# Attention of both layers reordered among its projections, and each weight unit's low half used last

## What is computed

```python
for i in range(2):
    h = rms_norm(x, attn_norm[i])
    c_q, c_kv, k_r, q_d, k_d, v_d, g_mla, g_dil = split(h @ w_in[i])
    o_mla = mla_attention(...)        # 8 heads, low-rank q and kv, rotary
    o_dil = dilated_mixer(q_d, k_d, v_d)   # 3 groups x 8 heads of 64, ALiBi
    merged = (sigmoid(g_mla) * (o_mla @ w_br_mla[i]) + sigmoid(g_dil) * (o_dil @ w_br_dil[i]))
    x = x + merged @ w_out[i]
    h = rms_norm(x, ffn_norm[i])
    x = x + (swiglu(h, ...) if i == 0 else moe_swiglu(h, ...))   # d_ff 3584; 8 experts, top 2
    h = rms_norm(x, ple_norm[i])
    x = x + sigmoid(h @ ple_w_gate[i]) * (p[i] @ ple_w_proj[i])
return rms_norm(x, final_norm)
```

## Time and profile before

| | |
|---|---|
| three runs | 2065.55 us median (2065.05 to 2072.18) |
| the profiled execution | 2059.12 us, of which the span of instructions 2057.4 us |
| mean granted TensorE clock | 0.959 |
| busy over the span | PE 95%, DVE 73%, ACT 60% |

### The profile page before, as it was taken

The page is one execution under the profiler, slowest core; times in us unless marked ns, Lnnn a source line. Parts: engine busy times, 40 slices in busy tenths (PEclk is TensorE's granted clock), DMA queues, the critical chain, the costliest instruction groups (busy, mean ns, idle before and its releaser), DMA issues.

```text
span 2057.4 us, 27403 instructions
## 1 busy us (share of the span) xinstructions
PE 1961.5 (95%) x9278; PEld 1633.5 (79%) x9278; DVE 1497.9 (73%) x1685; ACT 1242.8 (60%) x1543; POOL 68.5 (3%) x127
## 2 busy tenths in 40 slices
PE   6998999999999999999899999999999999999996
PEld 5887877788887887877688888888888888888875
DVE  4456447556666455545698999989999898998985
ACT  4545354444445544443577777777777777777764
POOL 2200001000001100001000000000000000000000
PEclk8999899999999997799799999999999999999998
DMA  6543114555554542124499998989989898998980
GB/s 252 192 183 110 54 62 169 194 183 183 184 183 167 213 160 75 42 81 141 185 359 349 352 369 329 367 338 353 371 324 366 339 355 342 352 368 340 351 324 31
DMA packets 70064, 498.61 MB, mean 242 GB/s; under 512 B 7872, under 2 KB 7872, under 8 KB 10096
## 3 DMA queue, kind: packets, MB, share of 16 engines
q1 hardware_dynamic: 68656, 493.39, 63.8%
q0 software_dynamic: 1344, 4.36, 0.7%
HBM read 496.67 MB, written 1.05 MB: 242 GB/s over the span
## 4 chain that ended last, share of the span: by engine, by line
PE 90%; DVE 3%; ACT 3%; issue 3%; DMA 1%; POOL 1%; ACTq 0%; DVEq 0%; SPq 0%; POOLq 0%
PE ps L1425 27%; PE ps L1427 26%; PE ps L1426 26%; PE ps L1562 2%; PE ps L1705 2%; PE ps L1544 1%; PE ps L1713 1%; DVE lo L925 1%; PE ps L1510 1%; ACT hi L554 1%; PE ps L1555 1%; PE ps L1533 0%; PE ps L1522 0%; ACT pT L682 0%; ACT pr L672 0%
## 5 line engine op out<-in xcount | busy, mean ns | idle before, releaser
L925 DVE TENSOR_TENSOR lo<-raw,hi 128x1024 fp32r<-128x1024 f32 (+1 forms) x936 | 1104.8, 1219 | 237.4 <-ACT hi L554 235.6
L554 ACT ACTIVATE hi<-raw 128x1024 fp32r<-128x1024 f32 (+1 forms) x936 | 969.1, 1053 | 395.3 <-PE ps L1427 381.6
L1425 PE MATMUL ps<-hi,hs_hi 128*128 128x512 f32 x896 | 360.6, 402 | 6.9 <-DVE lo L925 5.4
L1425 PE MATMUL ps<-hi,hT_hi 128*128 128x512 f32 (+1 forms) x832 | 344.2, 414 | 21.4 <-DVE lo L925 14.5
L1427 PE MATMUL ps<-hi,hs_lo 128*128 128x512 f32 x896 | 352.5, 393 | 0.0
L1426 PE MATMUL ps<-lo,hs_hi 128*128 128x512 f32 x896 | 349.9, 391 | 0.0
L1426 PE MATMUL ps<-lo,hT_hi 128*128 128x512 f32 (+1 forms) x832 | 335.9, 404 | 0.0
L1427 PE MATMUL ps<-hi,hT_lo 128*128 128x512 f32 (+1 forms) x832 | 335.3, 403 | 0.0
L1425 PEld LDWEIGHTS ps<-hi,hT_hi 128*128 128x128 f32 x832 | 166.8, 200 | 57.6 <-DVE lo L925 11.9
L1425 PEld LDWEIGHTS ps<-hi,hs_hi 128*128 128x128 f32 x896 | 169.1, 189 | 42.7 <-DVE lo L925 8.8
L1427 PEld LDWEIGHTS ps<-hi,hs_lo 128*128 128x128 f32 x896 | 168.9, 188 | 39.6
(11 more groups left out here) (270 smaller groups left out, 1866.4 us busy)
## 6 DMA issues: line engine op xcount, KB each, us to landing
raw<-in_stream SPq DMA_DIRECT2D x468, 1024.0 KB, 4.8
xs<-in_x SPq DMA_DIRECT2D x2, 512.0 KB, 7.0
gain<-in_ffn_norm POOLq DMA_DIRECT2D x2, 512.0 KB, 3.7
gain<-in_ple_norm POOLq DMA_DIRECT2D x2, 512.0 KB, 6.1
out_x<-hnat SPq DMA_DIRECT2D x4, 256.0 KB, 2.3
gain<-in_attn_norm SPq DMA_DIRECT2D x1, 512.0 KB, 5.2
pnat<-in_p POOLq DMA_DIRECT2D x2, 256.0 KB, 3.2
gain<-in_attn_norm POOLq DMA_DIRECT2D x1, 512.0 KB, 6.4
```

The lines of the kernel that those rows point to most:

```text
L554: a.activation(dst, src, ACT.Copy).then_inc(hi_done, 1)
L925: v.tensor_tensor(dst, src, h, ALU.subtract).then_inc(lo_done, 1)
L1425: pe.matmul(o, ah, wh[:, kk, :], start=(first and kk == 0), stop=False)
```

## The change

1. **Low half last.** `unit` waits for `hi_done`, does hi x hi and the low activation half for all k-tiles and blocks, then waits for `lo_done` and does the matmuls with the low weight half. The number of matmuls is the same.
2. **Attention reordered.** The six MLA batches move in between the units of the last three q/k groups, two per group, in banks of their own (scores 2 and 3, probabilities 7). These three groups now all use banks 0 and 1, and the rounds from 6 on use 4 and 5 alone. Of the gate and branch units, three stand ahead of the dilated loop and 16 in it, one in every dilated step but one (`FILL_AT`), where the MLA output is transposed (`OM_AT`). All gates use the bank pair 2 and 3. `exps(n)` waits for `normalise(n - 4)`, since `sums` has four places.
3. **Branches and merge.** The MLA branch units are fillers, the dilated output is transposed in two halves, the additions of the merge go from GpSimd to DVE (`merge`), and `w_out` starts when the first half of the merged rows is ready.
4. **Aligned regions.** `region` rounds its start up to 128 bytes. `omT`, `odT` and `merged` lie at other offsets.

```diff
-EV_OPS = [2] * 7 + [4, 4] + [2] * 9
-GATE_BANKS = (3, 7)
-BRANCH_BANKS = ((2, 6), (0, 1))
+EV_OPS = [2] * 7 + [4, 4] + [2] * 10
+GATE_BANKS = (2, 3)
+BRANCH_BANKS = ((2, 3), (0, 1), (6, 7), (2, 3))
...
-GATE_AT = {n + 2: n for n in range(4)}
-GATE_AT.update({NB_M + 2 + 2 * k: 4 + k for k in range(8)})
-GATE_AT[NB + 1] = 12
-
-SPLIT_AT = {2: 1, NB_M + 4: 2, NB_M + 8: 3}
+FILL_AT = {n: n - 3 for n in range(NB_M, NB_M + 13)}
+FILL_AT.update({NB_M + 14 + k: 16 + k for k in range(3)})
+OM_AT = NB_M + 13
+
+SPLIT_AT = {NB_M + 1: 1, NB_M + 4: 2, NB_M + 8: 3}
...
         def region(n):
+            top[0] = (top[0] + 127) // 128 * 128
...
-        sums = sb("sums", [P, 2, 4])
+        sums = sb("sums", [P, 4, 4])
...
                 def exps(n):
                     a.wait_ge(y.smax, n + 1)
-                    if n >= 2:
-                        a.wait_ge(y.oev, n - 1)
+                    if n >= 4:
+                        a.wait_ge(y.oev, n - 3)
...
+                for j in range(3, 6):
+                    u, n = b + U_Q + 4 * j, 2 * (j - 3)
+                    split_to(u + 6, **kw)
+                    exps(n)
+                    if n:
+                        pt_evac(n - 1)
+                    split_to(u + 7, **kw)
+                    chunk_evac(j)
+                    split_to(u + 8, **kw)
+                    exps(n + 1)
+                    pt_evac(n)
...
+                for n in range(NB_M, NB + 1):
+                    x = FILL_AT.get(n - 1, 0)
+                    if x % 4 == 3 and x < 16:
+                        gate_evac(x // 4, ACT.Copy, y.ev_act)
+                    if n < NB:
+                        exps(n)
+                    if n > NB_M:
+                        pt_evac(n - 1)
...
             def unit(u, dyn, l_hi, l_lo, dims, k0, outs, c0, first, last):
 
                 nk, w = dims
-                pe.wait_ge(lo_done, dyn + u + 1 + LO0)
+                pe.wait_ge(hi_done, dyn + u + 1)
...
                         pe.matmul(o, ah, wh[:, kk, :], start=(first and kk == 0), stop=False)
-                        pe.matmul(o, ah, wl[:, kk, :], start=False, stop=False)
-                        ins = pe.matmul(o, al, wh[:, kk, :], start=False, stop=(last and kk == nk - 1))
+                        pe.matmul(o, al, wh[:, kk, :], start=False, stop=False)
+                pe.wait_ge(lo_done, dyn + u + 1 + LO0)
+                for kk in range(nk):
+                    for t, bank in enumerate(outs):
+                        ins = pe.matmul(ps[:, bank, c0:c0 + w], l_hi[:, k0 + kk, P * t:P * t + P], wl[:, kk, :],
+                                        start=False, stop=(last and kk == nk - 1))
                 ins.then_inc(used, 1)
...
+                for j in range(3, 6):
+                    evacuated((10, 12, 13)[j - 3])
+                    for h in range(4):
+                        unit(b + U_Q + 4 * j + h, dyn, hT_hi, hT_lo, (2, CH), 2 * h, (0, 1), 0, h == 0, h == 3)
+                        if h == 2:
+                            turn_round(j + 3, "qk", j - 1)
+                        if h % 2 == 1:
+                            n = 2 * (j - 3) + h // 2
...
+                            scores(n)
+                            if n >= 1:
+                                turn_probs(n - 1)
+                            if n >= 2:
+                                values(n - 2)
+                pe.wait_ge(y.smax, NB_M)
+                fill_unit(0)
+                turn_probs(5)
+                values(4)
+                turn_round(9, "qk", 5)
+                fill_unit(1)
+                values(5)
+                fill_unit(2)
```

More of the change, by code:

```diff
@@ L653, in attn, with chunk_evac @@
                 a.wait_ge(y.rope_k, 1)
[L654 to L657, removed]
+                def chunk_evac(j):
+                    done(b + U_Q + 4 * j + 3)
                     if j >= 2:
                         a.wait_ge(y.tround, CHUNK_ROUND[j - 2] + 1)
+                    bank = 2 * ((9 + j) % 2) if j < 3 else 0
                     for t in range(T):
-                        a.activation(chunk[:, j % 2, t, :], ps[:, 2 * ((9 + j) % 2) + t, :], ACT.Copy,
+                        a.activation(chunk[:, j % 2, t, :], ps[:, bank + t, :], ACT.Copy,
                                      scale=rq8[:, i, t:t + 1] if j < 3 else col(y.n1, t)).then_inc(y.ev_act, 1)
@@ L705, in attn @@
                         pt_evac(n - 1)
[L706 to L711, removed]
+                    if n == OM_AT:
+                        a.wait_ge(y.otr, 1)
+                        a.activation(tok_blocks(omT_hi, 4), pair_blocks(2), ACT.Copy).then_inc(y.ohi, 1)
@@ L721, in attn @@
[L721 to L728, removed]
+                for k in range(2):
+                    a.wait_ge(y.otr, k + 2)
+                    a.activation(od_half(odT_hi, k), od_blocks(k), ACT.Copy).then_inc(y.ohi, 1)
@@ new lines, in attn @@
+                a.wait_ge(y.ev_act, EV_ACT[18])
+                for k in range(2):
+                    for t in range(T):
+                        a.activation(gates[:, k, t, :], gates[:, k, t, :], ACT.Sigmoid).then_inc(y.gsig, 1)
+                    split_to(b + U_BD + 4 + k, **kw)
+                his, banks = hT_groups(hT_hi)
+                for h in range(2):
+                    split_to(b + U_BD + 6 + 2 * h, **kw)
+                    for j in (2 * h, 2 * h + 1):
+                        a.wait_ge(y.mtr, j + 1)
+                        a.activation(his[j], banks[j], ACT.Copy).then_inc(y.mhi, 1)
@@ L1138, in attn @@
+                branch(0, 0)
+                split_to(b + U_BD + 4, dyn)
+                branch(1, 1)
+                split_to(b + U_BD + 5, dyn)
+                branch(2, 0)
+                merge(0)
+                split_to(b + U_BD + 6, dyn)
+                merged_rest(0)
+                split_to(b + U_BD + 7, dyn)
+                branch(3, 1)
+                merge(1)
+                split_to(b + U_BD + 8, dyn)
+                merged_rest(1)
                 split_to(b + U_O + 7, dyn)
@@ L1593, in attn @@
[L1593 to L1602 removed]
+                o_dil_turn(1)
+                fill_unit(19)
@@ L1603, in attn @@
+                pe.wait_ge(y.ev_vec, 4)
+                pe.wait_ge(y.mlo, 2)
+                for h in range(4):
+                    if h == 1:
+                        turn_tiles(merged, y.mtr, y.madd, 0, (2, 3))
+                    if h == 2:
+                        pe.wait_ge(y.mlo, 4)
+                    unit(b + U_O + h, dyn, hT_hi, hT_lo, (2, CH), 2 * h, (0, 1), 0, h == 0, h == 3)
                 pe.wait_ge(y.ev_vec, 8)
-                cols(b + U_O, dyn, hT_hi, hT_lo, (0, 1), ready=(y.mlo, 0))
```

281 lines of the change are left out of this document (168 added, 113 removed).

## The result

| | before | changed |
|---|---|---|
| median of 4 runs | 2065.3 us (2064.41 to 2072.18) | 2004.33 us (1999.91 to 2007.76) |
| ratio | | 0.9693, 95% interval 0.967 to 0.9717 |
| profiled execution, and its span | 2059.12, 2057.4 us | 2003.67, 2001.9 us |

The account below looks back on a forecast made before the run. PE was taken to bound the kernel, with idle time and lowered clock in attention. Attention 38, low half last 11.6 and alignment 9.1 sum to 58.7 us, taking 2065.55 to 2007 us; range 1980 to 2036.

Parts of the forecast that it names:

- Low half last, 11.6 us: Units that waited for lo start once hi is ready: 11.6 us saved, ends 6 and 18.
- slower rival: In every unit, the wait in the middle empties PE's queue: 103 us over 936 units, 2110 us in all; chance 0.04.
- Alignment, 9.1 us: Matmuls with weights in the regions: 4368 win 2.1 ns each once aligned, 9.1 us; ends 0 and 9.1.
- Attention, 38 us: Both layers' attention: upper bound 75 us, less 33 new idle time and 4 clock loss; ends 0 and 75.
- entry stall: Ahead of the first gate unit, PE waits for the last MLA batch's prep: 2.7 us.
- four gate evictions: In each layer's attention, PE waits for ACT to free the shared gate banks: 10 us in all.
- other lags on ACT: In the gate eviction's chain, further delays on ACT raise its time from 3.6 to 4.2 us.
- half microsecond named beside the pair's rounding: At gate evictions with a pair rounded in between: half a microsecond for the loop ACT and DVE are behind in.
- the branch unit, the tail and the merge: First MLA branch unit, last head's tail and merge: stalls of 1.4, 1.0 and 0.9 us.
- I leave 4 us of the 44.6: Attention's clock: of 44.6 us lost at lowered clock, only 4 us stay, judged by how often units come.
- the clock keeps falling: Attention: half of the 44.6 us clock loss stays, 18 us more than forecast, 2025 us; chance 0.16.
- rival of covered stalls: Attention: ACT and DVE keep ahead, new stalls vanish, nearly 75 us gained, 1970 us; chance 0.10.

Follow-up runs that it names:

- b1: Changed kernel with its regions not aligned, 192 bytes past a multiple of 256: 2028.25 us.
- a1: Kernel before the change with only the rounding of the regions to 128 bytes added: 2051.79 us, ratio 0.9928.
- b2: Changed kernel with raw, hi and lo 64 bytes further (192 past a multiple of 256), weights still aligned: 2040.42 us, ratio 0.9886.
- e1: Changed kernel with its regions at 64 bytes past a multiple of 256: 2012.5 us, ratio 0.9747.
- c2: a4 plus a shorter entry into the gates and the MLA output rounded ahead of exponentials and normalise: 1965.24 us, ratio 0.9514.
- a4: Changed kernel with ACT's gate eviction moved ahead, right behind the exponentials in the step of the group's last unit: 1986.41 us, ratio 0.9606.
- a2: Kernel before the change with only the new unit (wait for hi first, low weight half last): 2054.4 us, ratio 0.9943.
- after_again: The changed kernel itself, run again unchanged beside its variants: 2005.08 us.
- a3: Changed kernel with the unit of before (one wait for lo, low weight half in the middle): 2016.48 us, ratio 0.976.
- d1: Changed kernel with the old wait on the norm factors, exps(n) waiting for normalise(n - 2): 2026.87 us, ratio 0.9817.

## Why the prediction was right, and where it wasn't

The time was 2004 us against 2007, and the sum was right for the most part by its terms. That the two numbers lie so close is in part luck.

- **Low half last, 11.6 us.** Right: 11.8 alone, 11.4 in the changed kernel. The fulfilled wait in the middle of a unit costs nothing that shows (24 matmuls with `faT` keep 226.7 ns with one in each unit), and the slower rival had no base.
- **Alignment, 9.1 us.** Right for this pair of addresses: 7.6 us in the seven experts, where 7.4 was priced. The count left out `omT` and `odT`, 192 matmuls by the traces, 0.4 us (the expectation of b1 says 384). The Trainium skill ("TensorE: Matmul & The Clock Gate", section "Step-by-step: what each phase is for") has the load beside the matmul, and by that rule a load slowed by its address would have cost nothing; the trace is against it (7.6 us in a1). My picture of it, that the load is what slows, was only argued, and b2 shows it to be too narrow: the streamed operand does it too. The expectation for b1, 10 us, was less than half of the 23 measured: b1 put the regions 192 past a multiple of 256, and e1, at the 64 past of before, lost 7.4.
- **The two together in the experts.** 1.70 us per expert were priced (1.06 and 0.64). Gathers start at 1194.00 and 1317.87 us in the changed kernel, 123.87 apart, against 125.64 in before (1111.86 and 1237.50): 1.77.
- **Attention, 38 us.** Right in size, 33.2, by two errors against each other. *Idle time* was put at 16 us per layer and is 12.0. The entry stall was right (2.7). Of the four gate evictions 1.6, 3.3, 3.3 and 1.6 were named; 1.12, 2.65, 2.65 and 1.19 are there in layer 0. The 0.6 us of "other lags on ACT" (3.6 to 4.2) weren't there, and the half microsecond named beside the pair's rounding isn't in the 3.3 at all; the branch unit, the tail and the merge cost less. *The clock* was to cost 2 us per layer and cost 9.2 by the same reckoning, the lost share times the stretch. That reckoning counts slow clock also while PE stands: by the 165.1 us of PE's work in c2, 184.3 - 12.0 - 165.1 = 7.2 us is what it really cost. The forecast of 178 to 182 us for a stretch and 0.97 for its clock failed by that (184.3, 184.5, 0.95).
- **The step that failed** is "I leave 4 us of the 44.6". It took the clock to follow the mean density of units in the loop, one in about 5.8 us. In the traces it follows the stalls: full for 82 us on end in a4, where the gates no longer make PE wait, full throughout in c2, and half for one unit behind most of the stalls of the changed kernel, though not behind all. The stalls that I had listed just above should have carried that price too: 2.4 us for each unit at half clock. The rival "the clock keeps falling" put 22.3 us of clock loss in place of 4, since "each 3 us stall can start it"; 18.4 were there, reckoned the same way. So its step was nearer, and the profiled gain still came within 3.2 us of the forecast (55.5 against 58.7) because the stalls were some 8 us less than priced and the other stages gained 1.6 us more.
- **From the profiled execution to the median.** The forecast added to the new profiled time the 6.4 us by which the median of before lay above its profiled execution. In the changed kernel this difference is 0.7 us (2004.33 and 2003.67). So the profiled times differ by 3.2 us less than the sum, and the medians by 61.0 us, 2.3 more: the two misses are of opposite sign, and that is luck. The profiled execution of before was a fast one, at a clock of 0.959 where its 18 runs beside a1 have a median of 0.955. In a2, which has the attention of before, layer 0's stretch takes 206.0 us at 0.87, not 195.9 at 0.92.
- **A part without a price.** The late norm factors are a condition of the reordering, 21.8 us, and the prediction didn't speak of them. It had counted them in, unsaid, in the chain that it gave for the gate eviction: no step of it waits for the values on PE.
- The rival of covered stalls (1970 us) named a time that the reordering can reach, with the gates evicted first and two other moves: 1965.

## What to carry to other kernels

When a change spreads work among short steps, list for each engine what stands between a PSUM result and the operation that frees its bank, and put the eviction first; here that and two other moves that shorten what PE waits for (39.8 us in all, from the changed kernel to c2) were worth about twice what alignment and the order in the unit brought together. A PE stall has two prices, its own length and the unit at half clock that may follow, and both belong in the sum. Let every tile that a matmul streams or loads begin at a multiple of 128 bytes (0 and 128 past a multiple of 256 were tried, against 64 and 192), and look at the addresses again whenever a small tile ahead of them grows.

## What was not expected of the hardware

- A matmul of 128 x 512 in this format takes 226.7 ns with both operands at multiples of 128 bytes (128 past or at a multiple of 256 alike). With the weights 64 past a multiple of 256 it takes 228.8 to 229.2 ns, and 192 past 233.3. With the streamed operand 192 past and the weights aligned it takes 233.3 as well. The streamed operand at 64 past wasn't tried.
- The same duration of splits and of the 128-column `hn` matmuls (276 ns median in the changed kernel, b1, e1 and b2), whose tiles lie in the moved region too: only the wide matmuls feel the address.
- The clock's answer to a stall isn't fixed. The changed kernel has six stalls of 2.65 to 2.74 us in the attentions; a unit at half clock follows four of them, and the other two (before 253.60 and 768.89 us) nothing. Shorter ones had it as well: behind the stalls of 0.94 us before 282.06 and of 1.12 us before 786.98 the clock is 0.66 (282 to 287 and 787 to 792 us), while behind the 1.12 us before 202.09 it is full (187 to 222 us). In its other profiled execution (after_again) the same gate stall, again 2.65 us and ended at 252.16 us, was followed by half clock, while the entry's stall, with half clock in the first execution, went without. The same 10 us in the changed kernel and in that execution:

```profile
250.00:260.00 10.00, 7.35 (x48) 6.36 (x47) 4.92 (x10) 5.90 (x9) 0.00 (x0) 1.00 0.02 10
```
```profile
250.00:260.00 10.00, 7.84 (x34) 6.55 (x34) 2.40 (x7) 4.46 (x8) 0.00 (x0) 0.66 0.00 0
```

What decides it wasn't tried. It may be what the spread from run to run is made of: 8 us in the changed kernel and up to 16 in before, against 1.4 in c2, whose attentions have no stall left. But stalls alone don't make a spread: a3 and d1 have all of them, d1 longer ones, and their five runs spread over 2.2 and 1.6 us.
